# A chunked linear-recurrence scan: the chunk inverse built on 32-row blocks in place of 64-row ones

## The reference, cut to what matters

```
def step(s, inp):
    r_t, w_t, k_t, v_t, a_t, b_t = inp
    sa = jnp.einsum('bhij,bhj->bhi', s, a_t)
    s = s * w_t[:, :, None, :] + sa[..., None] * b_t[:, :, None, :] + v_t[..., None] * k_t[:, :, None, :]
    return s, jnp.einsum('bhij,bhj->bhi', s, r_t)
```

## Time and profile before

| what | us |
|---|---|
| median of 3 runs | 3266.66 (3264.73 to 3270.63) |
| the profiled execution | 3264.91 |
| its span, first to last instruction | 3263.3 |
| the scan, of that | some 228 (1177 to 1405) |
| TensorE busy, of the span | 3107.3 (95%) |
| VectorE busy | 1656.5 (51%) |
| ScalarE busy | 939.4 (29%) |
| GpSimd busy | 294.1 (9%) |

### The profile page before, as it was taken

How to read it: one execution, slowest core, us unless ns; L and a number is a source line. 1 busy time by engine, 2 the same in 40 slices (tenths; PEclk the granted TensorE clock), 3 DMA queues, 4 the chain that set the end, 5 groups by cost and what they waited for, 6 DMA issues and landing times. The chain is left out here.

```text
span 3263.3 us, 61887 instructions
## 1 busy us (share of the span) xinstructions
PE 3107.3 (95%) x25826; PEld 2937.6 (90%) x25826; DVE 1656.5 (51%) x2929; ACT 939.4 (29%) x1742; POOL 294.1 (9%) x326
## 2 busy tenths in 40 slices
PE   7999999998999989978898989999998999999998
PEld 6999999998999989837676669999998999999998
DVE  4454444546544746656654453343435554445545
ACT  5212122114211422244655352221244111111113
POOL 0000000004100212230002100000023000000003
PEclk8999999999999999988999999999999999999999
DMA  6111111103422220002013641112134111111103
GB/s 190 47 39 51 51 40 50 39 26 101 144 83 79 67 86 5 18 3 64 7 53 120 232 179 52 49 49 53 37 96 130 39 39 58 44 51 39 39 26 104
DMA packets 257468, 218.60 MB, mean 67 GB/s; under 512 B 41688, under 2 KB 235009, under 8 KB 256634
## 3 DMA queue, kind: packets, MB, share of 16 engines
q1 hardware_dynamic: 252410, 196.33, 19.6%
q0 software_dynamic: 3824, 19.47, 1.7%
q10 hardware_dynamic: 1040, 0.00, 0.0%
HBM read 179.81 MB, written 35.96 MB: 66 GB/s over the span
## 5 line engine op out<-in xcount | busy, mean ns | idle before, releaser
L1484 PE MATMUL banks<-XR,wR 128*128 128x344 f32 x6336 | 1004.8, 320 | 5.9 <-DVE rs L1598 4.3
L1484 PEld LDWEIGHTS banks<-XR,wR 128*128 128x128 f32 x6336 | 998.9, 188 | 6.5 <-issue 3.1
L1484 PE MATMUL banks<-hidR,wR 128*128 128x344 f32 x3168 | 511.1, 321 | 2.9 <-DVE tiles L1718 2.9
L1484 PEld LDWEIGHTS banks<-hidR,wR 128*128 128x128 f32 x3168 | 500.6, 188 | 9.2 <-DVE tiles L1718 4.7
L1567 ACT ACTIVATE sq<-sq 128x344 f32<-128x344 f32 x120 | 59.2, 493 | 927.1 <-DVE sq L1596 927.1
L1618 DVE TENSOR_TENSOR tiles<-tiles,banks 128x344 f32<-128x344 f32 x480 | 240.4, 511 | 166.1 <-PE banks L1484 165.2
L1095 PE MATMUL banks<-XR,pR 128*128 128x344 f32 (+1 forms) x1944 | 318.4, 325 | 3.6 <-DVE pR L2208 2.9
L1095 PEld LDWEIGHTS banks<-XR,pR 128*128 128x128 f32 (+1 forms) x1944 | 311.7, 191 | 10.2 <-issue 6.1
L1095 PE MATMUL banks<-XR,mg_gate 128*128 128x344 f32 x1728 | 283.3, 319 | 1.3 <-PEq L53 1.3
L1095 PEld LDWEIGHTS banks<-XR,mg_gate 128*128 128x128 f32 x1728 | 273.8, 188 | 1.6 <-issue 1.6
L1596 DVE TENSOR_TENSOR sq<-banks,shared 128x344 f32<-128x344 f32 x120 | 61.9, 516 | 365.7 <-PE banks L1484 365.6
(11 more groups left out here) (481 smaller groups left out, 3936.4 us busy)
## 6 DMA issues: line engine op xcount, KB each, us to landing
wraw<-in_ffn_down SPq DMA_DIRECT2D x22, 1024.0 KB, 4.8
wraw<-in_ffn_gate SPq DMA_DIRECT2D x43, 512.0 KB, 3.7
wraw<-in_ffn_up SPq DMA_DIRECT2D x43, 512.0 KB, 4.8
praw<-in_w_in SPq DMA_DIRECT2D x26, 512.0 KB, 4.2
tiles<-h_spill SPq DMA_DIRECT2D x9, 1376.0 KB, 6.9
sq<-in_w_in SPq DMA_DIRECT2D x24, 512.0 KB, 4.0
tiles<-in_cache_mla SPq DMA_DIRECT2D x64, 144.0 KB, 3.1
tiles<-in_cache_mla POOLq DMA_DIRECT2D x64, 144.0 KB, 3.2
```

The lines of the kernel that those rows point to most:

```text
L1484: ins = self.k.nc.tensor.matmul(out, wgt[:, a, cols], x(b)[:, grp(g)], start=first and n == 0, stop=last and n == 2)
```

## The change

The levels 2 to 16 never join rows across the middle of a chunk, so the change does them on the two diagonal 32 x 32 blocks of each 64 x 64 matrix. Tm, its transpose Tt, the masked parts, Y and both Z become 32 columns wide; on the partitions lie four blocks of 32 rows, and each product of a block is a call of its own. In place of "g3" `gram_blocks` makes the diagonal blocks of the Gram matrix in both orientations; ScalarE copies one of them (Gm), from which GpSimd now takes its masked parts. Level 16 writes the finished blocks into TT, whose other parts are zero from the start. Level 32 makes the one off-diagonal block, which ScalarE copies into TT's corner. In the order of the lists, `carried_state(b)`, W, U and S of chunk b each move one level back, S and its sum to level 32, and `output(b)` stands undivided behind the last `outer`.

```diff
+BLK = CH // 2
...
+    def piece(t, j, h, lo=0):
+
+        return t[BLK * j:BLK * (j + 1), h, lo:lo + BLK]
...
+            nc.gpsimd.memset(work[:, 0:4 * NU], 0.0).then_inc(zeroed.sem, 1)
             for p in range(NP):
...
-                for i, l in enumerate(LV[1:]):
+                for i, l in enumerate(LV[:-1]):
                     for s in R2:
-                        pe_s.wait(pool, ("Y", p, s, LV[i]))
-                        level(p, s, l)
+                        if i == 0:
+                            act_s.wait(pool, ("Gm", p, s))
+                        else:
+                            pe_s.wait(pool, ("Y", p, s, LV[i - 1]))
+                        pool_s.done(nc.gpsimd.tensor_tensor(NT_[s], Gm[s], k.level_mask[l], ALU.mult), ("level", p, s, l))
...
-                    if m == "g2":
-                        dve_s.wait(pe, ("T", p - 1, 1, LV[-1]))
+                    else:
+                        act_s.wait(pe, ("corner", p - 1, 1))
...
+            def gram_blocks(p):
...
+                for n in R2:
+                    for h in H4:
+                        for i in R2:
+                            for s in R2:
+                                for q in R2:
+                                    c = 2 * p + s
+                                    j = 2 * side(c, q) + i
...
+                                    ins = mm(piece(blocks(Gb[s], n * NB), j, h), lane(left, h, q, BLK * i, BLK),
+                                             lane(right, h, q, BLK * i, BLK))
+                pe_s.done(ins, ("blocks", p))
...
             def solved(c):
                 z, s = c // 2 % 2, c % 2
                 act_s.wait(pe, ("W", c))
-                dve_s.wait(pe, ("T", c // 2, s, LV[-1]))
+                act_s.wait(pe, ("corner", c // 2, s))
...
-                pe_s.done(both(lambda h, q: mm(lane(half(Yb[s], 0, CH), h, q), lane(NT_[s], h, q), lane(Tm[s], h, q))),
-                          ("Y", p, s, l))
+                if l < LV[-1]:
+                    pool_s.wait(pe, ("level", p, s, l))
+                for h in H4:
+                    for j in range(4) if l < LV[-1] else (1, 3):
+                        left = piece(NT_[s], j, h) if l < LV[-1] else piece(G1[p % 2][s], j - 1, h, BLK)
+                        ins = mm(piece(blocks(Yb[s], 0), j, h), left, piece(Tm[s], j if l < LV[-1] else j - 1, h))
+                pe_s.done(ins, ("Y", p, s, l))
...
-                if l < LV[-1]:
-                    both(lambda h, q: mm(lane(half(Zb[s], 0, CH), h, q), lane(TT[z][s], h, q), lane(Ym[s], h, q)))
-                pe_s.done(both(lambda h, q: mm(lane(half(Zb[s], NU, CH), h, q), lane(Ym[s], h, q), lane(TT[z][s], h, q))),
-                          ("Z", p, s, l))
+                for m in R2 if l < LV[-1] else (1,):
+                    for h in H4:
+                        for j in range(4) if l < LV[-1] else (1, 3):
+                            if l == LV[-1]:
+                                ins = mm(piece(blocks(Zb[s], NB), j - 1, h), piece(Ym[s], j, h), piece(TT[z][s], j, h, BLK))
+                            elif m:
+                                ins = mm(piece(blocks(Zb[s], NB), j, h), piece(Ym[s], j, h), piece(Tt[s], j, h))
+                            else:
+                                mm(piece(blocks(Zb[s], 0), j, h), piece(Tt[s], j, h), piece(Ym[s], j, h))
+                pe_s.done(ins, ("Z", p, s, l))
...
                         if l == 4:
+                            carried_state(b)
+                        if l == 8:
                             carried_values(b)
-                        if l == 8:
+                        if l == 16:
                             solved(b)
-                        if l == 16:
+                        if l == 32:
                             state(b)
-                        if l == 32:
-                            output(b, (0, 1))
...
-                            output(b, (2, 3))
+                            output(b, H4)
...
+                        copy(Gm[s], blocks(Gb[s], 0), ("Gm", p, s), ("blocks", p))
...
+                for s in R2 if this else ():
+                    pe_s.wait(act, ("Z", p, s, LV[-1]))
+                    for q in R2:
+                        at = slice(64 * q, 64 * q + BLK)
+                        ins = nc.scalar.activation(TT[z][s][at, :, BLK:CH], blocks(Zb[s], NB)[at], ACT.Copy)
+                    act_s.done(ins, ("corner", p, s))
+                if past:
+                    out(b)
...
+                        nc.vector.tensor_tensor(Tm[s], Tm[s], blocks(Zb[s], 0), ALU.add)
+                        if l < LV[-2]:
+                            ins = nc.vector.tensor_tensor(Tt[s], Tt[s], blocks(Zb[s], NB), ALU.add)
+                        else:
+                            for j in range(4):
+                                at = slice(BLK * j, BLK * (j + 1))
+                                lo = BLK * (j % 2)
+                                ins = nc.vector.tensor_tensor(TT[z][s][at, :, lo:lo + BLK], Tt[s][at], blocks(Zb[s], NB)[at], ALU.add)
+                        dve_s.done(ins, ("T", p, s, l))
```

More of the change, by code:

```diff
@@ L298, in four, with two @@
         return [[view(area, at + (2 * z + s) * RT * c, c) for s in R2] for z in R2]
-    def two(at):
-        return [view(work, at + s * NU, CH) for s in R2]
+    def two(at, c=CH):
+        return [view(work, at + s * RT * c, c) for s in R2]
     G1, G2 = four(room, 0, 2 * CH), four(room, 8 * NU, 2 * CH)
@@ L307, in rwkv_scan @@
     TT = four(work, 0, CH)
-    Tm, NT_, Ym, Wm, Um = (two((4 + 2 * m) * NU) for m in range(5))
+    Wm, Um = (two((4 + 2 * m) * NU) for m in R2)
+    Tm, Tt, Gm, NT_, Ym = (two(8 * NU + 2 * m * NB, BLK) for m in range(5))
     ST = [view(work, 14 * NU, CH), k.ST, k.st_rows]
     Yb, Zb, Wb, Sb, Ob = (0, 1), (2, 3), 5, 6, 7
+    Gb = (4, Ob)
     def half(b, lo, c):
@@ L345, in rwkv_scan @@
-            dve_steps += [("T", p, s, l) for s in R2] if this else []
+            act_steps += {8: [("W", b), ("O", a)], 16: [("U", b)]}.get(l, []) if past else []
+            dve_steps += [("sum", a), ("state", a)] if past and l == 2 else []
+            dve_steps += [("T", p, s, l) for s in R2] if this and l < LV[-1] else []
+            dve_steps += [("sum", b), ("state", b)] if past and l == LV[-1] else []
+        act_steps += ([("corner", p, s) for s in R2] if this else []) + ([("O", b)] if past else [])
@@ L528, in _ @@
                     gram(p, "g1")
-                    gram(p, "g3")
+                    gram_blocks(p)
                     gram(p, "g2")
@@ L589, in one, with out @@
                     copy(out, x, step, step)
+                def out(c):
+                    one(k.C[:, 0:4, c * CH:(c + 1) * CH], half(Ob, 0, CH), ("O", c))
+                if this:
+                    for s in R2:
+                        copy(Gm[s], blocks(Gb[s], 0), ("Gm", p, s), ("blocks", p))
                 if past:
@@ L599, in _ @@
                     for s in R2:
-                        copy(Km[z][s], half((4, Ob)[s], 0, CH), ("K", p, s), ("K", p))
+                        copy(Km[z][s], half(Gb[s], 0, CH), ("K", p, s), ("K", p))
                 for l in LV:
@@ L640, in _ @@
                     for s in R2:
[L641 to L644, removed]
+                        dve_s.wait(dve, ("Tt", p, s))
+                        dve_s.done(nc.vector.tensor_tensor(Tt[s], Tt[s], k.ident4, ALU.add), ("first", p, s))
                     pe_s.wait(dve, ("g2", p))
@@ L648, in _ @@
                 for i, l in enumerate(LV):
-                    if past and l in (2, 16):
-                        state(a if l == 2 else b)
-                    for s in R2 if this else ():
+                    if past and l == LV[0]:
+                        state(a)
+                    for s in R2 if this and l < LV[-1] else ():
                         pe_s.wait(dve, ("Z", p, s, l))
[L653 to L656, removed]
+                        dve_s.wait(dve, ("T", p, s, LV[i - 1]) if i else ("first", p, s))
+                        nc.vector.tensor_tensor(Tm[s], Tm[s], blocks(Zb[s], 0), ALU.add)
+                        if l < LV[-2]:
+                            ins = nc.vector.tensor_tensor(Tt[s], Tt[s], blocks(Zb[s], NB), ALU.add)
+                        else:
+                            for j in range(4):
[3 more added lines that the diff above has]
+                        dve_s.done(ins, ("T", p, s, l))
                     if past and this:
                         sample.on_dve(dve, 3 if l == LV[-1] else 2)
+                if past:
+                    state(b)
 class SampleStep:
@@ L4657, in build @@
         k.gram = shared[:, 0:2 * CH]
[L4658 removed]
+        k.masks = shared[:, 2 * CH:2 * CH + 7 * BLK].rearrange("p (i c) -> p i c", i=7)
         k.ST, k.st_rows = (shared[:, 10 * CH + i * RT * RN:10 * CH + (i + 1) * RT * RN].rearrange("p (h c) -> p h c", h=RT)
```

79 lines of the change are left out of this document (35 added, 44 removed).

## The result

The changed kernel takes 3384.06 us (median of 4 runs, 3381.23 to 3391.62) where the kernel before takes 3265.72 (median of 4 runs): 1.036 times as long, 95% interval 1.034 to 1.038, 118 us slower. The forecast was 3368, 103 above the profiled execution of the kernel before. The profiled execution took 3386.08 us.

A forecast was written before the change was run, and what follows sets the result against it. TensorE in the scan was taken to wait for its own code: 3264.9 + 94 (rounds two to eight) + 7.5 (first round) + 0.7 (last piece) = 3367, with 0.5 to 1 for other engines 3368 us; range 3345 to 3400.

The forecast's parts named there:

- What bounds the kernel: In the scan's rounds: TensorE waits for its own code, one packet for each 256 instructions or 128 load and matmul pairs.
- The number of packets: In rounds two to eight: 688 calls in place of 448, so 10.75 packets a round.
- The price of a packet: In the scan: 3.72 us each, bounds 3.5 and 3.95; 40.0 us a round, +94 us over seven rounds.
- closer than 3.4 us: Sign for the scan's packets: the forecast is wrong if they come closer than this.
- What of the work isn't hidden: In the scan's rounds: no portion of 128 pairs works 3.7 us, so TensorE's work hides behind the code's arrival.
- part (3): ScalarE, VectorE, GpSimd: shorter copies, sums and masks; zero, at most 0.3 us a round where level 32 waits for quarter sums.
- The work under the cover: TensorE's array work: 8 ns a small pair, changes of tile shape 0.12 us each; 2.9 us a round less, hidden.
- Order and waits: Corner copies, Gm and the later state sum: zero as long as code arrives late; undone, up to 0.7 us a round.
- The ends of the scan: First round: 8.9 packets plus 1.5 us for delays, +7.5 us; last piece: half an output stands ahead, +0.7 us.
- Packets hidden: Rival: the scan's gaps have another cause or fetches overlap, so the work saved is the gain: 3244 us; chance 0.09.
- A floor for small matmuls: Rival: each 32-column pair in the levels takes 25 ns, with code hidden: 3349 us; chance 0.03.
- The clock falls as well: Rival: TensorE's clock drops in the rounds, 64-row portions last 5 to 6 us, +4.5 a round: 3399 us; chance 0.12.

The follow-up runs named there:

- the useless calls: Kernel before with 240 one-column products of no use added a round (688 calls in all): 3388.69 us, ratio 1.037.
- without g3: Kernel before without the 16 g3 products a round, Tm starting as VectorE's transpose of TT (432 calls): 3262.4 us, ratio 0.9984.
- the turned kernel: Kernel before without g3 and, in levels 2 to 16, Tm made by VectorE's transpose of TT (368 calls): 3244.58 us, ratio 0.9928.
- the clock back up: Changed kernel with the products of the levels, but level 32's outer, made 64 columns wide, same number of instructions: 3381.37 us, ratio 1.035.
- the new order alone: Kernel before with only the reordering of the older chunks' products, no instructions added: 3267.57 us, ratio 1.0002.

## Why the prediction was right, and where it was off

**What bounds the kernel** was read rightly: in most of a round TensorE has less work than its code takes to arrive. The stops, the packets and the kernels with 448 to 688 calls follow it, and the useless calls show it without any of the change's own parts. Below 448 calls it isn't shown: without g3 the rounds of the profile didn't get shorter, and the turned kernel has array work and VectorE's waits near its code's time.

**The number of packets.** 10.75 a round were forecast, "some 75" from round two to eight; 77 were moved from 1214.38 to 1516, and 29 more in all against 30 counted.

**The price of a packet** is the mis-sized term. It was taken at 3.72 us from one run with quick work; the portions in a row from 1311.84 on come every 3.83, which is 10.75 x 0.11 = 1.2 us a round more. The bounds of 3.5 and 3.95 held this pace, but not the rounds: 43.1 us in 10.75 portions are 4.01 each. The mean of 3.80 in the kernel before was at hand and would have given 3374. In the DMA records a packet itself lasts between 0.88 and 1.5 us, and the distances between packets were spread over 3.35 to 4.08 before the change, so one run's 3.70 was a poor guide to a mean. What makes a packet long or short is open. The sign "closer than 3.4 us" was badly set for the same reason, because the kernel before has distances of 3.35.

**What of the work isn't hidden.** The prediction said that no portion works as long as its packet's time. In the fourth round two do: 4.29 us with the waits for the quarter sums (0.30 + 0.96 us; part (3) allowed 0.3), and 5.40 us of 64-row pairs without a stop at a granted clock of 0.56. All seven distances over 4.3 us between packets of rounds two to seven lie within 8 us of the end of a round, where these portions stand. With the clock back up and the quarter sums' waits still there a round is 41.3, so by this one run most of what lies above the pace goes with the clock: 40.0 + 1.2 + 1.8 = 43.0, and 43.1 was measured. A portion costs its packet's turn or its own work with its waits, whichever is longer. That this is also why a packet more costs 4.4 us between two kernels (34.2 to 43.1 us for two), more than the pace of 3.83, is argued, not shown.

**The work under the cover** was as forecast: the 96 matmuls at 1312.91 start 9.1 ns apart on average, where 8 were taken, and the 113 at 1319.91, where the granted clock is 0.50, 13.5. It hides, as said. A change from 32 x 32 to 64 x 64 tiles takes 0.12 us from start to start at the full clock and back 0.15 (medians of 21 and 25), near what the prediction took. In the groups by shape of the changed kernel from 1214.38 to 1516, beside the earlier trace rows, the sums and copies became as much shorter as part (3) allowed, and stayed without effect:

```profile
L386 POOL TENSOR_TENSOR tiles<-tiles,shared 128x128 f32<-128x128 f32 x56 | 26.0, 475 | 270.4 <-ACT tiles L609 141.4 <-PE banks L406 129.0
L609 ACT ACTIVATE tiles<-banks 128x128 f32<-128x128 f32 x84 | 22.4, 278 | 153.4 <-PE banks L406 152.6
...
L695 DVE TENSOR_TENSOR tiles<-tiles,banks 128x128 f32<-128x128 f32 x56 | 16.1, 288 | 116.4 <-PE banks L406 115.8 <-DVE tiles L664 0.2
```

**Order and waits** at zero: the new order alone is 1.0002 (0.9992 to 1.0012), and among the waits of the changed kernel's TensorE none is for a corner copy (L652).

**The ends of the scan.** The first round was forecast at +7.5 and gave +11.8; its granted clock is 0.68, and the weight loads' stops for "issue" in it went from 8.6 us in 7 to 17.7 in 9, up to 3.5 us inside the round, where the transfers run. What makes them long wasn't taken apart. The eighth round with the last piece was forecast at 13.4 + 0.7 and gave +12.8. These misses, +4.3 and -1.3, and 3.1 us a round in six rounds are 21.6; the earlier start, the 1.1 us given back behind the scan and the 0.5 to 1 for (3) bring it to the 18 us between the profiled 3386 and 3368.

**The rivals.** *Packets hidden* (3244) is out: the useless calls alone make the kernel some 120 us slower. *A floor for small matmuls* (3349) is out: pairs start 9 ns apart. Nor is it a price of each instruction: 96 of them start that close together, and then nothing starts for 2.00 us. *The clock falls as well* (3399) came true in its event and only in part in its price: the granted clock is 0.69 to 0.80 in rounds two to seven, a mix of the 2.4 and 1.2 GHz levels, where TensorE works 30 to 33 of 42 to 44 us; but a round with the clock back up is only 1.8 us shorter, where 4.5 was priced. The 5 to 6 us that it gave a portion of 64-row pairs at half the clock were right (5.40 at 1339.11), but the stretch shown in order of time has one such portion, and most others at half the clock still work less than 3.83 us and hide it. Of the 3.1 us a round that the forecast lacked, some 1.8 go with the clock by that run; in the whole time the kernel with the clock back up is 2.7 us faster, within the spread of the runs.

## To carry to other kernels

Where TensorE's weight loads stop for "issue" every 128 pairs, count its instructions, not its columns: here each 256 of them cost 3.8 to 4.4 us, and halving the columns of levels 2 to 16 with twice the calls there costs 118 us. Fewer calls can be a way out: those that another engine took over (a transpose on VectorE, 445 ns in place of 8 calls) gave 24 us, though array work went with them. A stage whose engine looks 93% busy (24.6 of 26.5 us) can be held up by the arrival of its code, and busy time alone does not show it.

## What was not expected of the hardware

The loop of one packet is mostly waiting and not transfer. In the three turns from 1311.84 on it is 1.0 to 1.4 us from the portion's start to the packet, 1.3 to 1.4 us for the packet by the DMA records, and 1.3 to 1.5 us from its end to the next portion's start. Neither twice the columns nor the clock shortens it: with more columns portions still stop (71.0 us in 63), and the packets of rounds two to seven begin 3.81 us apart in the median. The Trainium skill, "Runtime: NRT & Kernel Launch", section "Instruction fetch mechanics", calls the cost of these refills mostly hidden; the packets' size agrees with it (2.88 MB in 176), and the cost doesn't: 81.7 us of stops in 302 us.

The granted clock rose from 0.69 to 0.80 up to 0.95 to 1.00 when the same number of instructions had twice the columns, with TensorE's busy time near the same in the rows (31 against 32 us a round). It gave the rounds 1.8 us and the kernel nothing that can be measured.
